# Where four small SBUF buffers lie: the stationary operand of the feed-forwards' down projection

## The chip, the core and the metric

The kernel is one program on one core of a Trainium2 chip. The metric is the device time of one execution in microseconds (us), lower is better. Before the change the median of three runs is 3006.59 us (3006.22 to 3006.69).

## The reference: what is computed

The reference is a stack of transformer layers on 256 tokens of width 1024, all in float32. Four layers of a first block (sliding-window attention, gated linear attention, RWKV-7, sliding-window attention) and one layer of a second block (dilated plus grouped attention) each hold one token mixer and two feed-forwards, so there are ten feed-forwards in all:

```
def swiglu(x, w_in, w_out):
    gate, up = jnp.split(x @ w_in, 2, axis=-1)
    return (jax.nn.silu(gate) * up) @ w_out       # 1024 -> 2 x 2816 -> 1024

for layer in range(DEPTH):
    ff = swiglu(rmsnorm(h, g[0]), ffn_w_in[layer, 0], ffn_w_out[layer, 0])
    h = h + 0.5 * rmsnorm(ff, g[1])
    ...                                           # mixer, then a second feed-forward
```

The second block's feed-forwards are the same with three separate matrices (`ffn1_w1`, `ffn1_w3`, `ffn1_w2` and `ffn2_...`).

## The kernel before, in words

Every engine has a program written out by hand; the order of its instructions is the order of the Python code, and semaphores tie the engines together. Nothing is scheduled or planned by a tool.

**Split numbers.** TensorE multiplies float32r operands. To keep float32 accuracy each operand `a` is split in two float32r parts, `a = high + low`, and a product is taken as high·high + high·low + low·high. Weights arrive by DMA in `raw0` to `raw3`; ScalarE rounds a slot to `high0`/`high1` (`split_high`, L333), VectorE makes `low0`/`low1` as the rest (`split_low`, L337). The turned activation `x_parts` has, for each of the eight 128-row blocks of the model width, 256 tokens of high part and behind them 256 tokens of low part.

**A feed-forward** (`ffn_pe`, `ffn_act`, `ffn_dve`) walks 22 blocks of 128 hidden columns in units q = 0 to 22. Unit q first makes the gate and the up columns of block q: for each of 2 x 8 steps one matmul of 512 columns (L413; weights `high` stationary, `x_parts` moving, both parts at once) and one of 256 columns (L414; `low` stationary, the high part moving). Then it does the down projection of block q-1: for 2 token tiles and 2 halves of the output three matmuls of 512 columns each (L433, L434, L435), 12 in all. There the activation is the stationary operand and the weights are moving:

```
nc.tensor.matmul(o, hid_h[b][:, tok], H[:, w], start=(q == 1), stop=False)
nc.tensor.matmul(o, hid_h[b][:, tok], L[:, w], start=False, stop=False)
last = nc.tensor.matmul(o, hid_l[b][:, tok], H[:, w], start=False, stop=(q == FB))
```

`hid_h[b]` and `hid_l[b]` are the two parts of the activated block, 128 partitions x 256 tokens, two buffers of each (b = (q-1) % 2). VectorE writes them once per unit, `hid_h` at L503 and `hid_l` at L505; it waits first for the down projection two blocks back, and TensorE waits for L505 before L433. Beside `hid_*` nothing here is touched by the change. The mixers don't use `hid_*`.

**Projections of the mixers** (`proj_pe`, L589) have two layouts. With feature-major output the weights are stationary. Token-major ones take `x_parts` as stationary and the weights as moving; the output projections among them stream 512 columns in the same order of three terms (high·high, high·low, low·high) as the down projection does.

**Where buffers lie.** `sb(...)` hands out SBUF from low to high addresses in the order of the calls, without gaps but for a rounding up to 32 bytes. Per partition, in bytes, as the built program has it:

```
buffer            before    after    remainder by 128: before, after
raw0..raw3         16512    same     0
high0, high1       65664    same     0
low0, low1         90240    same     0
x_parts           131200    same     0   (16384 bytes, to 147584)
hid_h0            157888    147584   64, 0
hid_h1            158912    148608   64, 0
hid_l0            159936    149632   64, 0
hid_l1            160960    150656   64, 0
gain0, gain1      147584    151680   0, 0
gain_columns0     155776    159872   0, 0
silu, hidden      155840    159936   64, 64
ident             161984    same     64
mix               167264    same     96
```

Divided by 512, `x_parts` leaves 128, `hid_*` left 192 before and leave 128 after: the 512-byte line of the change's name is counted from the first buffer, which starts at 16512.

Of the kernel before, what the change touches and what calls it, by code (L numbers as in the profile page):

```python
# [6 lines left out]
F32R = mybir.dt.float32r  # L7
# [4 lines left out]
P = 128  # L12
SEQ = 256
# [90 lines left out]
def build(nc, io, out, stages):  # L104
# [49 lines left out]
    with ctx:  # L154
        def sb(name, shape, dt=F32):
            return ctx.enter_context(nc.sbuf_tensor(name, shape, dt))
# [8 lines left out]
        y = sb("y", [P, NT, D])  # L165
        x_parts = sb("x_parts", [P, KB, 2 * SEQ], F32R)
        xh, xl = x_parts[:, :, 0:SEQ], x_parts[:, :, SEQ:2 * SEQ]
        gain = [sb(f"gain{i}", [P, D]) for i in range(2)]
        gain_columns = [sb(f"gain_columns{i}", [P, KB]) for i in range(2)]
        silu = sb("silu", [P, SEQ])  # L170
        hidden = sb("hidden", [P, SEQ])
        hid_h = [sb(f"hid_h{i}", [P, SEQ], F32R) for i in range(2)]
        hid_l = [sb(f"hid_l{i}", [P, SEQ], F32R) for i in range(2)]
        ident = sb("ident", [P, P])
        ones = sb("ones", [P, P])
        squares = sb("squares", [P, 2 * NT])
# [3197 lines left out]
```

## Time and profile before

| | value |
|---|---|
| median of three runs | 3006.59 us (3006.22 to 3006.69) |
| time of the profiled execution | 3007.35 us |
| span of the profiled execution | 3005.4 us |
| TensorE busy with matmuls | 2882.7 us, 96% of the span |
| VectorE, ScalarE, GpSimd busy | 70%, 48%, 3% |
| mean share of the 16 DMA engines | about half (51.7% for the weights' queue) |
| mean granted TensorE clock | 0.988 of full |

The span goes from the first to the last instruction; the profiled execution's own time is 1.95 us longer. In the trace, PE is TensorE's matmul side and PEld its loading of the stationary operand, which runs beside the matmul before it. Records of matmuls overlap, since they are pipelined: a matmul's length includes a latency that the next one hides. What a matmul costs in a dense row is therefore read from start to start, and the time given for one record only by comparison with another of the same shape.

### The profile page before, as it was taken

The numbers are of one execution on the slowest core, as the hardware profiler recorded it, in microseconds if no ns is written. First come the engines' busy times: TensorE is split into PE (matmuls) and PEld (weight loads), VectorE is DVE, ScalarE is ACT, GpSimd is POOL, SyncE is SP. The second block draws the span as 40 slices with busy tenths as digits, with TensorE's granted clock in tenths as the row PEclk, the third lists the DMA queues.
The fourth block names the chain that finished last, engine by engine and source line by source line (L and its number), as shares of the span: only waits on it lengthen the run. The fifth ranks groups of instructions, "written<-read, shape, count | busy, mean of one in ns | idle before, by whom it ended". The sixth has DMA issues, their size and how long they took to land.

```text
span 3005.4 us, 44680 instructions
## 1 busy us (share of the span) xinstructions
PE 2882.7 (96%) x17202; PEld 2491.9 (83%) x17202; DVE 2102.8 (70%) x3035; ACT 1448.9 (48%) x1865; POOL 84.4 (3%) x94
## 2 busy tenths in 40 slices
PE   8998999999999999999999999998999999989998
PEld 7887787888888888888988878876887889978887
DVE  6767677776767777767767777766777775565676
ACT  5445545445544444563444454455445444444443
POOL 0000000000000000100120000000000000000000
PEclk9999999999999999999999999999999999999999
DMA  8643564663456566431016656643656656533662
GB/s 241 207 115 127 173 196 142 210 191 114 133 179 196 157 189 207 121 121 50 1 53 186 196 153 198 185 126 120 189 182 175 189 159 183 183 116 129 200 195 84
DMA packets 614848, 471.24 MB, mean 157 GB/s; under 512 B 40545, under 2 KB 572385, under 8 KB 614708
## 3 DMA queue, kind: packets, MB, share of 16 engines
q1 hardware_dynamic: 614564, 469.31, 51.7%
q8 instruction: 95, 1.56, 0.2%
q14 instruction: 45, 0.37, 0.0%
q10 hardware_dynamic: 144, 0.00, 0.0%
HBM read 466.37 MB, written 1.84 MB: 156 GB/s over the span
## 4 chain that ended last, share of the span: by engine, by line
PE 84%; DVE 8%; ACT 5%; issue 2%; DMA 0%; SPq 0%; PEldq 0%; ACTq 0%; DVEq 0%; PEld 0%
PE pair_bank L413 26%; PE pair_bank L414 14%; PE pair_bank L589 11%; PE out_banks L433 7%; PE out_banks L435 7%; PE out_banks L434 7%; PE out_banks L589 2%; DVE low L337 2%; ACT high L333 2%; PE pair_bank L406 1%; PE pair_bank L2200 1%; PE pair_bank L2188 1%; DVE h L733 1%; PE pair_bank L2184 1%; DVE y L723 1%
## 5 line engine op out<-in xcount | busy, mean ns | idle before, releaser
L337 DVE TENSOR_TENSOR low<-raw,high 128x3072 fp32r<-128x3072 f32 (+2 forms) x328 | 934.7, 2850 | 603.7 <-ACT high L333 602.9
L413 PE MATMUL pair_bank<-x_parts,high 128*128 128x512 f32 x3360 | 1179.1, 393 | 4.4 <-issue 2.4
L414 PE MATMUL pair_bank<-x_parts,low 128*128 128x256 f32 x3520 | 961.9, 280 | 0.0
L333 ACT ACTIVATE high<-raw 128x3072 fp32r<-128x3072 f32 (+2 forms) x328 | 774.0, 2360 | 255.2 <-PE out_banks L435 154.0
L413 PEld LDWEIGHTS pair_bank<-x_parts,high 128*128 128x128 f32 x3360 | 629.6, 187 | 150.3 <-issue 7.8
L414 PEld LDWEIGHTS pair_bank<-x_parts,low 128*128 128x128 f32 x3520 | 655.1, 189 | 10.7 <-DVE low L337 1.1
L463 ACT ACTIVATE sq_scratch<-pair_bank 128x512 f32<-128x512 f32 x220 | 131.6, 598 | 559.1 <-PE pair_bank L414 559.1
L433 PE MATMUL out_banks<-high,hid_h 128*128 128x512 f32 x880 | 348.5, 396 | 9.5 <-DVE hid_l L505 9.5
L434 PE MATMUL out_banks<-low,hid_h 128*128 128x512 f32 x880 | 347.9, 395 | 0.0
L435 PE MATMUL out_banks<-high,hid_l 128*128 128x512 f32 x880 | 347.8, 395 | 0.0
L589 PE MATMUL pair_bank<-high,x_parts 128*128 128x256 f32 x1216 | 232.1, 289 | 4.6 <-DVE x_parts L786 1.6
L589 PE MATMUL pair_bank<-x_parts,high 128*128 128x256 f32 (+2 forms) x1088 | 204.9, 290 | 12.8 <-DVE x_parts L786 5.2
L433 PEld LDWEIGHTS out_banks<-high,hid_h 128*128 128x128 f32 x880 | 165.2, 188 | 52.7 <-issue 13.6
L493 DVE TENSOR_TENSOR sq_scratch<-sq_scratch,pair_bank 128x256 f32<-128x256 f32 x440 | 183.7, 417 | 26.5 <-ACT sq_scratch L463 21.3
L589 PEld LDWEIGHTS pair_bank<-high,x_parts 128*128 128x128 f32 x1216 | 195.6, 195 | 7.0 <-DVE low L337 3.5
L465 ACT ACTIVATE silu<-sq_scratch 128x256 f32<-128x256 f32 x220 | 92.0, 418 | 222.8 <-DVE sq_scratch L495 222.6
L435 PEld LDWEIGHTS out_banks<-high,hid_l 128*128 128x128 f32 x880 | 165.4, 188 | 39.7
L495 DVE TENSOR_TENSOR sq_scratch<-sq_scratch,y 128x256 f32<-128x256 f32 x440 | 187.3, 426 | 15.0
L434 PEld LDWEIGHTS out_banks<-low,hid_h 128*128 128x128 f32 x880 | 165.3, 188 | 29.5
L589 PEld LDWEIGHTS pair_bank<-x_parts,high 128*128 128x128 f32 (+2 forms) x1088 | 171.5, 194 | 17.9 <-DVE low L337 10.1
L589 PE MATMUL pair_bank<-low,x_parts 128*128 128x256 f32 x608 | 173.6, 286 | 0.0
L589 PE MATMUL pair_bank<-x_parts,low 128*128 128x256 f32 (+2 forms) x544 | 156.1, 287 | 0.0
(374 smaller groups left out, 3060.6 us busy)
## 6 DMA issues: line engine op xcount, KB each, us to landing
raw<-in_ffn_w_in_dram SPq DMA_DIRECT2D x352, 512.0 KB
raw<-in_ffn_w_out_dram SPq DMA_DIRECT2D x176, 512.0 KB
raw<-in_ffn_w_dram SPq DMA_DIRECT2D x132, 512.0 KB
raw<-in_w_in_dram SPq DMA_DIRECT2D x32, 1024.0 KB
raw<-in_gla_w_in_dram SPq DMA_DIRECT2D x12, 1024.0 KB
raw<-in_rwkv_w_rkv_dram SPq DMA_DIRECT2D x12, 1024.0 KB
raw<-in_swa_w_qkv_dram SPq DMA_DIRECT2D x10, 1024.0 KB
raw<-in_swa_w_o_dram SPq DMA_DIRECT2D x8, 1024.0 KB
```

The lines of the kernel that those rows point to most:

```text
L333: nc.scalar.activation(high[u % SPLIT][:, lo:w], raw[u % RAW][:, lo:w], ACT.Copy).then_inc(high_ready, count)
L337: nc.vector.tensor_tensor(low[u % SPLIT][:, lo:w], raw[u % RAW][:, lo:w], high[u % SPLIT][:, lo:w].bitcast(F32), ALU.subtract).then_inc(we ...
L413: nc.tensor.matmul(o, H[:, w], x_parts[:, k, :], start=(k == 0), stop=False)
L414: last = nc.tensor.matmul(o[:, 0:SEQ], L[:, w], xh[:, k, :], start=False, stop=(k == KB - 1))
L433: nc.tensor.matmul(o, hid_h[b][:, tok], H[:, w], start=(q == 1), stop=False)
L434: nc.tensor.matmul(o, hid_h[b][:, tok], L[:, w], start=False, stop=False)
L435: last = nc.tensor.matmul(o, hid_l[b][:, tok], H[:, w], start=False, stop=(q == FB))
L463: nc.scalar.activation(lows[:, :, :], halves[:, :, SEQ:2 * SEQ], ACT.Copy).then_inc(lows_copied, 1)
L465: nc.scalar.activation(silu[:, :], sums[:, 0, :], ACT.Silu).then_inc(silu_ready, 1)
L493: nc.vector.tensor_tensor(sums[:, n, :], lows[:, n, :], halves[:, n, 0:SEQ], ALU.add).then_inc(sums_made, 1)
L495: nc.vector.tensor_tensor(sums[:, n, :], sums[:, n, :], scale_rows, ALU.mult).then_inc(sums_ready if n == 0 else sums_made, 1)
L589: last = nc.tensor.matmul(o, a, b, start=(j == 0 and opens), stop=(j == len(terms) - 1 and closes))
```

## The change

Four declarations stand in another place. No instruction, no order, no wait and no size differs: on each of the five engines the rows of the two programs are the same, and only the addresses inside them differ.

```
--- before.py
+++ after.py
@@ -165,12 +165,12 @@
         y = sb("y", [P, NT, D])
         x_parts = sb("x_parts", [P, KB, 2 * SEQ], F32R)
         xh, xl = x_parts[:, :, 0:SEQ], x_parts[:, :, SEQ:2 * SEQ]
+        hid_h = [sb(f"hid_h{i}", [P, SEQ], F32R) for i in range(2)]
+        hid_l = [sb(f"hid_l{i}", [P, SEQ], F32R) for i in range(2)]
         gain = [sb(f"gain{i}", [P, D]) for i in range(2)]
         gain_columns = [sb(f"gain_columns{i}", [P, KB]) for i in range(2)]
         silu = sb("silu", [P, SEQ])
         hidden = sb("hidden", [P, SEQ])
-        hid_h = [sb(f"hid_h{i}", [P, SEQ], F32R) for i in range(2)]
-        hid_l = [sb(f"hid_l{i}", [P, SEQ], F32R) for i in range(2)]
         ident = sb("ident", [P, P])
         ones = sb("ones", [P, P])
         squares = sb("squares", [P, 2 * NT])
```

So `hid_*` come 10304 bytes lower, directly behind `x_parts`; `gain0`, `gain1`, the gain columns, `silu` and `hidden` go up by 4096 bytes, which changes neither their remainder by 128 nor that by 512; everything else stays.

## Rows read from the trace of the kernel before

**Rows 1.** The page: busy times, then by line the chain that ended last.

```profile
PE 2882.7 (96%) x17202; PEld 2491.9 (83%) x17202; DVE 2102.8 (70%) x3035; ACT 1448.9 (48%) x1865; POOL 84.4 (3%) x94
...
PE pair_bank L413 26%; PE pair_bank L414 14%; PE pair_bank L589 11%; PE out_banks L433 7%; PE out_banks L435 7%; PE out_banks L434 7%; PE out_banks L589 2%; DVE low L337 2%; ACT high L333 2%; PE pair_bank L406 1%; PE pair_bank L2200 1%; PE pair_bank L2188 1%; DVE h L733 1%; PE pair_bank L2184 1%; DVE y L723 1%
```

**Rows 2.** Windows of one unit and of 19 units: TensorE busy, granted clock.

```profile
core 0: us, PE busy (x) PEld busy (x) DVE busy (x) ACT busy (x) POOL busy (x), PEclk, DMA share, GB/s
60.00:68.35 8.35, 8.35 (x46) 7.10 (x45) 6.07 (x8) 3.85 (x4) 0.00 (x0) 1.00 0.61 188
...
834.46:850.08 15.62, 15.62 (x70) 12.94 (x69) 7.80 (x5) 7.70 (x8) 0.00 (x0) 1.00 0.68 208
...
341.04:499.76 158.72, 158.72 (x837) 135.63 (x836) 117.39 (x157) 72.29 (x58) 0.00 (x0) 1.00 0.60 182
```

**Rows 3.** Timeline of TensorE in the first feed-forward: start, length, what.

```profile
63.47 0.39 PE L433 MATMUL out_banks<-high,hid_h 128*128 128x512 f32 x1
63.70 0.39 PE L434 MATMUL out_banks<-low,hid_h 128*128 128x512 f32 x1
...
66.27 0.40 PE L413 MATMUL pair_bank<-x_parts,high 128*128 128x512 f32 x1
66.50 0.27 PE L414 MATMUL pair_bank<-x_parts,low 128*128 128x256 f32 x1
66.61 0.40 PE L413 MATMUL pair_bank<-x_parts,high 128*128 128x512 f32 x1
...
71.82 0.39 PE L433 MATMUL out_banks<-high,hid_h 128*128 128x512 f32 x1
```

**Rows 4.** The same view in an output projection, `x_parts` stationary.

```profile
838.12 0.62 PE L589 MATMUL out_banks<-high,x_parts 128*128 128x512 f32 x2
838.57 0.39 PE L589 MATMUL out_banks<-low,x_parts 128*128 128x512 f32 x1
838.80 0.62 PE L589 MATMUL out_banks<-high,x_parts 128*128 128x512 f32 x2
...
849.00 0.61 PE L589 MATMUL out_banks<-high,x_parts 128*128 128x512 f32 x2
```

**Rows 5.** Instructions by tile: count, then length in ns, min/median/max.

```profile
L433 PEld LDWEIGHTS out_banks<-high,hid_h x880: 186/188/188, 29.9 to 2992.9; 128*128 128x128 f32 x176
L433 PE MATMUL out_banks<-high,hid_h x880: 391/394/476, 30.0 to 2993.1; 128*128 128x512 f32 x176
...
L589 PEld LDWEIGHTS out_banks<-high,x_parts x128: 186/188/330, 826.2 to 1586.2; 128*128 128x128 f32 x128
L589 PE MATMUL out_banks<-high,x_parts x128: 387/389/764, 826.2 to 1586.4; 128*128 128x512 f32 x128
```

**Rows 6.** Timeline of RWKV: plain float32 matmuls, stationary in `raw`, then in `mix`.

```profile
1394.76 1.06 PE L2188 MATMUL pair_bank<-raw 128*128 128x128 f32 x8
...
1416.93 1.06 PE L2188 MATMUL pair_bank<-mix 128*128 128x128 f32 x8
```

**Rows 7.** Timeline of a unit near a feed-forward's end: splitting, then the writes of `hid_*`.

```profile
492.06 2.77 ACT L333 ACTIVATE high<-raw 128x3072 fp32r<-128x3072 f32 x1 [0.90 <-PE out_banks L435]
...
494.87 3.36 DVE L337 TENSOR_TENSOR low<-raw,high 128x3072 fp32r<-128x3072 f32 x1 [2.11 <-ACT high L333]
...
500.16 0.39 PE L413 MATMUL pair_bank<-x_parts,high 128*128 128x512 f32 x1
500.36 0.29 DVE L503 CAST hid_h<-hidden 128x256 fp32r<-128x256 f32 x1
...
500.68 0.42 DVE L505 TENSOR_TENSOR hid_l<-hidden,hid_h 128x256 fp32r<-128x256 f32 x1
```

**Rows 8.** Waits of TensorE over the kernel: us in total, times, longest.

```profile
PE out_banks L433 <- DVE hid_l L505: 9.5, 10, 1.1
```

**Rows 9.** Timeline of a feed-forward's last two down projections.

```profile
505.71 0.39 PE L433 MATMUL out_banks<-high,hid_h 128*128 128x512 f32 x1
505.91 0.60 ACT L463 ACTIVATE sq_scratch<-pair_bank 128x512 f32<-128x512 f32 x1 [2.62 <-PE pair_bank L414]
...
509.61 0.47 PE L433 MATMUL out_banks<-high,hid_h 128*128 128x512 f32 x1 [0.93 <-DVE hid_l L505]
```

More of the change, by code:

```diff
@@ L167, in build @@
         xh, xl = x_parts[:, :, 0:SEQ], x_parts[:, :, SEQ:2 * SEQ]
+        hid_h = [sb(f"hid_h{i}", [P, SEQ], F32R) for i in range(2)]
+        hid_l = [sb(f"hid_l{i}", [P, SEQ], F32R) for i in range(2)]
         gain = [sb(f"gain{i}", [P, D]) for i in range(2)]
@@ L171, in build @@
         hidden = sb("hidden", [P, SEQ])
-        hid_h = [sb(f"hid_h{i}", [P, SEQ], F32R) for i in range(2)]
-        hid_l = [sb(f"hid_l{i}", [P, SEQ], F32R) for i in range(2)]
         ident = sb("ident", [P, P])
```

## The prediction

> **What bounds the kernel now.** I read the page's busy times and its chain first. TensorE is busy 96% of the span, and the chain of work that ended last is TensorE for 84%: gate and up matmuls 40% (L413, L414), the down projection 21% (L433 to L435, 7% each) [rows 1]. Then the windows: inside a feed-forward a unit takes 158.72 / 19 = 8.354 us, TensorE has no gap in it, VectorE is busy 117.39 / 158.72 = 74% and the clock is granted in full, 2.4 GHz [rows 2]. So a unit lasts as long as its 44 matmuls, and the question is what one costs from start to start. The timeline gives it: the 12 down matmuls go from 63.47 to 66.27, which is 2.80 / 12 = 233.3 ns each; the 16 pairs of gate and up from 66.27 to 71.82, 5.55 / 16 = 347 ns for 512 and 256 columns together [rows 3].
>
> The view that decides is the same timeline in a mixer's output projection. It streams 512 columns of weights too, with the same three terms in the same order, but its stationary operand is `x_parts`: 48 matmuls from 838.12 to 849.00, 10.88 / 48 = 226.7 ns each, at the same full clock [rows 4, 2]. The difference is 6.7 ns, which is 16 clocks of 2.4 GHz. The records by tile say it again from another side: with `x_parts` a 512-column matmul has min/median 387/389 ns, with `hid_h` 391/394, while the loads of the stationary operand are recorded alike, 188 ns [rows 5]. The pairs fit the smaller figure: 512 + 32 and 256 + 32 clocks are 832 clocks, 346.7 ns, as measured; 512 + 32 clocks are 226.7 ns; the down projection needs 512 + 48. In pairs and output projection every stationary operand begins at a multiple of 128 bytes. `hid_*` begin 64 bytes behind one.
>
> **The change, part by part.**
>
> *The stationary loads of the down projection.* They get the remainder that `x_parts` has, by 128 and by 512. If the address makes the 16 clocks, a down matmul costs 226.7 instead of 233.3 ns. Per unit 12 x 6.67 = 80 ns, and the unit goes from 8.354 to 8.274 us. There are 880 records of L433 [rows 5], four to a block of 12 matmuls, so 220 blocks, 22 to each of the ten feed-forwards.
>
> *What of it is on the path.* In 21 blocks of 22 the next work of TensorE stands ready behind the down projection. The block before the last is different: after it TensorE waits for the last `hid_l`, ten times, 9.5 us in total [rows 8]. That wait ends with VectorE, whose chain starts from the last gate and up matmul (ScalarE at 505.91), ahead of the down block, and ends at 509.46; TensorE starts at 509.61 [rows 9]. A shorter block there only lengthens the wait. So 210 blocks count: 210 x 80 ns = 16.8 us.
>
> *What could be late next.* ScalarE can split the next slot only when L435 has freed one, and both ends move together. In the unit shown ScalarE starts at 492.06, VectorE ends the low part at 494.87 + 3.36 = 498.23, and TensorE wants it at 500.16: 1.9 us of room, against 0.08 us that go [rows 7]. The hidden block is ready at 500.68 + 0.42 = 501.1 and is wanted after the 5.55 us of pairs, at 505.7 [rows 7, 9]. The weights' rate rises by 1%, from 182 GB/s with the DMA engines 60% busy [rows 2]. None of them comes near.
>
> *The other moved buffers.* `gain*`, `silu` and `hidden` keep their remainders, and they are read and written by VectorE and ScalarE beside a TensorE that is the bound. I put them at 0, with at most 0.3 us either way: the feed-forwards' tails are the only place where such an instruction is waited for, three in each of the ten (L499, L503, L505), and with 10 ns on each that is 0.3 us.
>
> *Bounds of the saving.* The trace has no float32r matmul with `hid_*` elsewhere, so the cost after is bounded by the nearest rows. From below: 226.7 ns, the output projection's. From above: 233.3 ns, as now. Between them stands the pitch from a 512-column L413 to its L414, 66.27 to 66.50, 230 ns [rows 3]; but the pair as a whole needs the 32 + 32 clocks, so I take 226.7. Outside these ends a little more could come: the pitches into the block (L414 to L433) and out of it also change by a few ns, at most 10 ns in each of 210, 2.1 us more.
>
> Sum: 16.8 us. The profiled execution took 3007.35 us with a span of 3005.4, so it would be 2990.5 and 2988.6. It lies 0.8 us above the median of the runs; from the median 3006.6 - 16.8 = **2989.8 us**, 0.56% less.
>
> *A page against it.* The trace shows 233.3 and 226.7 ns for one shape at one clock [rows 3, 4]. The Trainium skill, "SBUF — State Buffer", Specifications (TRN2), gives SBUF cachelines of 16 bytes as the grain at which an access pays for crossing; 64 is a multiple of 16, so by that rule the old and the new place are equally good and the time stays. "TensorE: Matmul & The Clock Gate", LDWEIGHTS (loading the stationary operand), has the load cost go by its columns alone, again with no address in it; and Back-to-back issue gap gives about 215.8 ns for 512 columns at full clock, which neither row reaches (no run here shows that value). What such an indifference would do here is the first rival.
>
> **The rivals.**
>
> *1. The address does not matter; the 16 clocks come from how the down projection is built.* It changes the output bank after every third matmul, the output projection after 24; it runs in a loop, the other doesn't; its stationary operand is written by VectorE shortly before. For it: in plain float32 the remainder shows nothing, eight matmuls with the stationary operand in `raw` (remainder 0) and eight with it in `mix` (96) take the same 1.06 us [rows 6]. Against it: those are another kind of matmul, about 112 ns for 128 columns; the pairs run in the same loop at 32 clocks over their columns; and a cost of the bank change would stand at every third matmul, but the first to the second (63.47 to 63.70, no change of bank between) is no shorter than 230 ns either. Time: 3006.6 us.
>
> *2. Half of it.* The down projection in the loop has its own floor at the 230 ns of L413 [rows 3]: 210 x 12 x 3.3 ns = 8.3 us, 2998.3 us. Against it stands that this 230 is followed by 117.
>
> *3. Slower: VectorE now writes next to what TensorE streams.* VectorE writes `hid_h` and `hid_l` (0.29 + 0.42 us) just when TensorE has begun the pairs and streams `x_parts` [rows 7], and now these buffers adjoin. If a write near by slows the stream, 0.71 us of every unit are exposed, 156 us over 220 units. It turns the sign from 80 / 710 = 11% of slowing on; at 20% it costs 31 us and the time is 3006.6 + 31 - 17 = 3021 us. Against it: for 3.36 us of a unit VectorE writes `low`, whose buffers adjoin each other and `high`, while TensorE loads from them, and TensorE stays without a gap [rows 2, 7].
>
> *4. The change doesn't do what it says.* The buffers do not start at a multiple of 512 bytes but 128 behind one. If a full line were needed nothing would move; but `x_parts` has the same remainder and runs at 226.7 ns, so this has little weight and goes into rival 1.
>
> **How the numbers follow.** The forecast has 0.75: one kind of matmul, one shape, one clock, and only the stationary operand's place in common with the change. Rival 1 (with 4) has 0.12, rival 2 0.07, rival 3 0.06. The forecast's own range is 2987 to 2992 (2.1 us more at the low end; at the high end as much, should one block in eight be held by something that I don't see). The range needs 8 in 10, so it takes in rival 2 as well: 2986 to 3000. A difference of 0.2%, 6 us, is about what a measurement tells here: faster 0.82, the same 0.12, slower 0.06.
>
> **What would show it.** In the changed profile L433 to L435 have a median near 389 ns instead of 394, their starts lie 0.227 us apart, and 12 take 2.72 us; the loads stay at 188 ns; 19 units take 157.2 us instead of 158.7; the wait for the last `hid_l` rises from 9.5 to about 10.3 us; L413, L414 and L589 stay. If the pitch stays at 233 ns the address is not the cause. If the pitch falls but the pairs' pitch rises above 347 ns in their first 0.7 us, rival 3 is at work. If the pitch falls to 227 and the time doesn't follow, one of the waits that I called far away is near.

## The result, and the profile after

The changed kernel takes 3014.12 us (median of 12 runs, 3008.74 to 3016.7) against 3006.23 us (12 runs); the ratio is 1.0029 with an interval of 1.0022 to 1.0036. It is 0.29% slower, where 0.56% faster was forecast, and outside the range.

The page after, against [rows 1]: busy times, then two groups of its fifth part.

```profile
PE 2889.4 (96%) x17202; PEld 2495.0 (83%) x17202; DVE 2104.7 (70%) x3035; ACT 1449.5 (48%) x1865; POOL 84.6 (3%) x94
...
L413 PE MATMUL pair_bank<-x_parts,high 128*128 128x512 f32 x3360 | 1196.7, 399 | 4.8 <-issue 2.3
...
L433 PE MATMUL out_banks<-high,hid_h 128*128 128x512 f32 x880 | 345.7, 393 | 10.0 <-DVE hid_l L505 10.0
```

The same two groups of the page of before:

```profile
L413 PE MATMUL pair_bank<-x_parts,high 128*128 128x512 f32 x3360 | 1179.1, 393 | 4.4 <-issue 2.4
...
L433 PE MATMUL out_banks<-high,hid_h 128*128 128x512 f32 x880 | 348.5, 396 | 9.5 <-DVE hid_l L505 9.5
```

So the down projection's matmuls got shorter and the gate and up matmuls, which the change doesn't touch, longer. By tile, against [rows 5], the down matmul moved as forecast:

```profile
L433 PEld LDWEIGHTS out_banks<-high,hid_h x880: 186/188/188, 29.7 to 2999.8; 128*128 128x128 f32 x176
L433 PE MATMUL out_banks<-high,hid_h x880: 387/389/470, 29.9 to 3000.0; 128*128 128x512 f32 x176
```

The windows after, against [rows 2], one unit of the first feed-forward and 19 of the second: 8.39 us, and 159.35 / 19 = 8.387 us, at the full clock.

```profile
60.00:68.39 8.39, 8.39 (x46) 7.16 (x45) 6.11 (x8) 3.85 (x4) 0.00 (x0) 1.00 0.63 190
342.59:501.94 159.35, 159.25 (x837) 135.79 (x837) 117.53 (x158) 72.31 (x58) 0.00 (x0) 1.00 0.60 182
```

The timeline of one unit after, against [rows 3], has it all:

```profile
367.95 0.39 PE L413 MATMUL pair_bank<-x_parts,high 128*128 128x512 f32 x1
368.18 0.28 PE L414 MATMUL pair_bank<-x_parts,low 128*128 128x256 f32 x1
368.29 0.40 PE L413 MATMUL pair_bank<-x_parts,high 128*128 128x512 f32 x1
...
369.00 0.40 PE L413 MATMUL pair_bank<-x_parts,high 128*128 128x512 f32 x1
369.24 0.28 PE L414 MATMUL pair_bank<-x_parts,low 128*128 128x256 f32 x1
369.35 0.40 PE L413 MATMUL pair_bank<-x_parts,high 128*128 128x512 f32 x1
...
373.59 0.40 PE L433 MATMUL out_banks<-high,hid_h 128*128 128x512 f32 x1
373.82 0.40 PE L434 MATMUL out_banks<-low,hid_h 128*128 128x512 f32 x1
...
374.98 0.39 PE L433 MATMUL out_banks<-high,hid_h 128*128 128x512 f32 x1
...
376.34 0.39 PE L413 MATMUL pair_bank<-x_parts,high 128*128 128x512 f32 x1
```

From 374.98 to 376.34 six down matmuls take 1.36 us, 226.7 ns each: the forecast pitch. But the first six behind the pairs take 1.39 us, 232 ns each. All 12 take 2.75 us instead of 2.80. The 16 pairs, 367.95 to 373.59, take 5.64 us instead of 5.55: 352.5 ns a pair, with a 512-column matmul of 0.24 us in every third pair (369.00 to 369.24). Per unit: 51 ns won, 85 lost, 34 ns net; over 210 units 7.1 us, against 7.9 us measured.

That slow pace of the pairs was already in the trace of before. Its timeline in unit q = 2 of the third feed-forward:

```profile
537.15 0.40 PE L413 MATMUL pair_bank<-x_parts,high 128*128 128x512 f32 x1
...
542.10 0.40 PE L413 MATMUL pair_bank<-x_parts,high 128*128 128x512 f32 x1
```

Fourteen pairs in 4.95 us, 353.6 ns each, where [rows 3] have 347. Unit q = 2 of three more of the ten feed-forwards, and q = 1 of six, run at it too. From q = 3 on the pairs of all ten are at 347 ns. So one stretch of code, at one set of addresses and at one clock, has two paces.

The changed kernel's trace shows the opposite step. In its second feed-forward the pairs of q = 2 still have the fast pace, and those of q = 3 the slow one:

```profile
343.23 0.40 PE L413 MATMUL pair_bank<-x_parts,high 128*128 128x512 f32 x1
...
348.43 0.39 PE L433 MATMUL out_banks<-high,hid_h 128*128 128x512 f32 x1
...
351.18 0.39 PE L413 MATMUL pair_bank<-x_parts,high 128*128 128x512 f32 x1
...
356.82 0.40 PE L433 MATMUL out_banks<-high,hid_h 128*128 128x512 f32 x1
```

Fifteen pairs in 5.20 us are 346.7 ns each; sixteen in 5.64 us are 352.5. Between them stands one down projection, the first in which TensorE doesn't wait. Seven of its ten feed-forwards have q = 2 at the fast pace, and in all ten every unit from q = 3 on is slow. In the first two units, where TensorE still waits between pairs and down projection, either pace occurs in both kernels; from q = 3 on the layout decides.

### The profile page after: what moved, and what is told of

It reads as the page before. It is cut to its first block, busy times and chain, and to the rows that moved or that the text cites. A ratio compares the mean times of both kernels' runs of the same rounds, so it can differ in the third digit from the quotient of the medians.

```text
span 3012.2 us, 44680 instructions
## 1 busy us (share of the span) xinstructions
PE 2889.4 (96%) x17202; PEld 2495.0 (83%) x17202; DVE 2104.7 (70%) x3035; ACT 1449.5 (48%) x1865; POOL 84.6 (3%) x94
## 4 chain that ended last, share of the span: by engine, by line
PE 83%; DVE 9%; ACT 5%; issue 2%; DMA 0%; SPq 0%; PEldq 0%; ACTq 0%; DVEq 0%; PEld 0%
PE pair_bank L413 26%; PE pair_bank L414 14%; PE pair_bank L589 11%; PE out_banks L433 6%; PE out_banks L434 6%; PE out_banks L435 6%; PE out_banks L589 2%; DVE low L337 2%; ACT high L333 2%; PE pair_bank L406 1%; PE pair_bank L2200 1%; PE pair_bank L2188 1%; DVE h L733 1%; PE pair_bank L2184 1%; DVE y L723 1%
## 5 line engine op out<-in xcount | busy, mean ns | idle before, releaser
L413 PE MATMUL pair_bank<-x_parts,high 128*128 128x512 f32 x3360 | 1196.7, 399 | 4.8 <-issue 2.3
L414 PE MATMUL pair_bank<-x_parts,low 128*128 128x256 f32 x3520 | 964.5, 281 | 0.0
L413 PEld LDWEIGHTS pair_bank<-x_parts,high 128*128 128x128 f32 x3360 | 631.9, 188 | 163.5 <-issue 8.3
L414 PEld LDWEIGHTS pair_bank<-x_parts,low 128*128 128x128 f32 x3520 | 655.4, 189 | 9.0 <-DVE low L337 1.1
L433 PE MATMUL out_banks<-high,hid_h 128*128 128x512 f32 x880 | 345.7, 393 | 10.0 <-DVE hid_l L505 10.0
L589 PE MATMUL pair_bank<-high,x_parts 128*128 128x256 f32 x1216 | 232.9, 289 | 4.6 <-DVE x_parts L786 1.6
L589 PE MATMUL pair_bank<-x_parts,high 128*128 128x256 f32 (+2 forms) x1088 | 206.3, 291 | 12.8 <-DVE x_parts L786 5.2
L433 PEld LDWEIGHTS out_banks<-high,hid_h 128*128 128x128 f32 x880 | 165.2, 188 | 52.3 <-issue 14.0
L589 PEld LDWEIGHTS pair_bank<-high,x_parts 128*128 128x128 f32 x1216 | 196.2, 195 | 7.1 <-DVE low L337 3.5
L589 PEld LDWEIGHTS pair_bank<-x_parts,high 128*128 128x128 f32 (+2 forms) x1088 | 172.8, 195 | 18.0 <-DVE low L337 10.1
L589 PE MATMUL pair_bank<-low,x_parts 128*128 128x256 f32 x608 | 174.0, 286 | 0.0
L589 PE MATMUL pair_bank<-x_parts,low 128*128 128x256 f32 (+2 forms) x544 | 156.8, 288 | 0.0
```

Source lines behind the costliest of these rows:

```text
L413: nc.tensor.matmul(o, H[:, w], x_parts[:, k, :], start=(k == 0), stop=False)
L414: last = nc.tensor.matmul(o[:, 0:SEQ], L[:, w], xh[:, k, :], start=False, stop=(k == KB - 1))
L589: last = nc.tensor.matmul(o, a, b, start=(j == 0 and opens), stop=(j == len(terms) - 1 and closes))
```

## The experiments

All but e5 and e6 only reorder declarations; the program is otherwise the one before. Remainders are by 512 bytes. Two operands are called in step when they leave the same remainder, and out of step when they don't. `gain_columns` (64 bytes) serves as the spacer. "Down" is from the first L433 of a unit to the next L413, "pairs" from there to the next L433; both are medians over 180 units, "unit" the mean over 190, from the starts in each trace. They repeat within 0.01 us per unit where two kernels have the same remainders (before and e2, changed and e1, e3 and e11, e16 and e17), much better than whole runs: the span without 190 units (mixers and edges) lay between 1411 and 1424 us in these profiles. Two numbers stand where the units alternate; in e7 half of the units of either parity have each. The last column is the ratio to the kernel before with its 95% interval, or the time in us.

| kernel | hid_h | hid_l | high | low, x_parts | down, us | pairs, us | unit, us | time |
|---|---|---|---|---|---|---|---|---|
| before | 192 | 192 | 128 | 128 | 2.798 | 5.555 | 8.353 | 3006.2 |
| changed | 128 | 128 | 128 | 128 | 2.747 | 5.640 | 8.387 | ratio 1.0029 |
| e1 | 128 | 128 | 128 | 128 | 2.747 | 5.640 | 8.388 | 1.0023 (1.0014 to 1.0033) |
| e2 | 192 | 192 | 128 | 128 | 2.798 | 5.555 | 8.351 | 0.9998 (0.9988 to 1.0007) |
| e3 | 128 | 192 | 128 | 128 | 2.770 | 5.550 | 8.320 | 0.9991 (0.9981 to 1.0001) |
| e4 | 192 | 128 | 128 | 128 | 2.802, 2.777 | 5.552, 5.550 | 8.339 | 0.9993 (0.9984 to 1.0003) |
| e5 | 128 | 128, 192 | 128 | 128 | 2.777 | 5.550 | 8.327 | 0.9991 (0.9982 to 1.0) |
| e6 | 192, 128 | 128 | 128 | 128 | 2.793 | 5.640 | 8.434 | 3023.85, one run |
| e7 | 160, 224 | 160, 224 | 128 | 128 | 2.80 to 2.81 | 5.55 or 5.65 | 8.405 | 3022.4, one run |
| e8 | 256 | 256 | 128 | 128 | 2.776, 2.796 | 5.644, 5.551 | 8.383 | 3012.25, one run |
| e9 | 192 | 192 | 192 | 192 | 2.747 | 5.640 | 8.387 | 3009.13, one run |
| e10 | 192 | 192 | 128 | 128, 192 | 2.803 | 5.643 | 8.445 | 3017.59, one run |
| e11 | 128 | 192 | 128 | 128 | 2.770 | 5.550 | 8.320 | 0.9986 (0.9977 to 0.9995) |
| e12 | 192 | 128 | 192 | 128 | 2.774 | 5.446 | 8.221 | 0.9917 (0.9903 to 0.9931) |
| e13 | 128 | 128 | 192 | 128 | 2.789, 2.804 | 5.597, 5.450 | 8.317 | 3001.57, one run |
| e14 | 128 | 128 | 128 | 192, 128 | 2.784, 2.779 | 5.550, 5.653 | 8.386 | 3007.86, one run |
| e15 | 192 | 192 | 192 | 128 | 2.784 | 5.609 | 8.393 | 1.0026 (1.0015 to 1.0037) |
| e16, e17 | 128 | 192 | 192 | 128 | 2.767 | 5.439 | 8.207 | 0.99 (0.9884 to 0.9917) |

(The two remainders of e5 and e6 are those of the first and the second token tile, those of e7 of its two buffers, those of e10 and e14 of low and x_parts. e16 is one run, 2975.76 us; the ratio is e17's.)

**Place or remainder: e1 and e2.** Theory A: the pairs' pace is handed on by the down projection's loads. Theory B, rival 3 of the prediction: `hid_*` next to `x_parts` disturb.

```
e1_far_aligned, from before      e2_near_64, from before
   x_parts                          x_parts
   gain                          +  gain_columns
-  gain_columns                  +  hid_h, hid_l
   silu, hidden, hid_h, hid_l       gain
+  gain_columns                  -  gain_columns
                                    silu, hidden
                                 -  hid_h, hid_l
```

> The gain columns are declared behind hid_*, so hid_* stay 10 KB from x_parts (157824) but begin at a multiple of 128 bytes. In the changed kernel a down matmul fell from 233 to about 227 ns (once five matmuls had passed), but the pairs of gate and up behind it rose from 347 to 352.5 ns, all 16 alike; the unit went from 8.354 to 8.387 us. Theory A (the pace of the pairs is carried over from the down matmuls ahead of them: the misaligned loads had put TensorE's loading and streaming in a favourable step): the place doesn't matter, only the remainder, so this is as the changed kernel: unit 8.387 us, about 3014 us. Theory B (hid_* next to x_parts disturbs the stream of x_parts): down 227 and pairs 347, unit 8.27 us, about 2990 us.

> The gain columns (64 bytes) are declared between x_parts and hid_*: hid_* are next to x_parts (147648) but begin 64 bytes behind a multiple of 128, as in the kernel before. Theory A: as the kernel before, down 233, pairs 347, unit 8.354 us, about 3006 us. Theory B: down 233 and pairs 352.5, unit about 8.43 us, about 3023 us.

Both came out as A has it, each to 2 ns per unit of the kernel that it should equal: far away but in step is as slow as the changed kernel, adjoining but out of step is as before. That refutes rival 3.

**Which loads set the pace: e3 to e6.** In e3 and e4 the spacer stands between the two parts, behind `x_parts`:

```
e3_low_part_64:   x_parts, hid_h, gain_columns, hid_l, gain, silu, hidden
e4_high_part_64:  x_parts, hid_l, gain_columns, hid_h, gain, silu, hidden
```

> Behind x_parts come hid_h (multiple of 128), then the gain columns, then hid_l (64 behind one). Of each three down matmuls one has a misaligned load, and it is the last before the pairs. Theory A, if the last load before the pairs sets their step: pairs 347, down 8 x 6.7 ns shorter, unit 8.30 us, about 2995 us. Theory A, if the step needs several such loads in a row: pairs 352.5, unit about 8.41 us, 3019 us. Theory B: pairs 352.5 in any case, 3019 us.

> As the one before with the parts exchanged: hid_l at a multiple of 128, hid_h 64 behind one; two of three down matmuls have a misaligned load, the last before the pairs has an aligned one. Theory A, if the last load sets the step: pairs 352.5, down 4 x 6.7 ns shorter than before, unit about 8.41 us, 3019 us. Theory A, if most of the loads do: pairs 347, unit 8.33 us, 3001 us. Theory B: 3019 us.

In both the pairs kept 347 ns. e3's unit fell to 8.320 us, somewhat more than half of the way to the 8.30 expected, and its time is 3003.42 us where 2995 was expected. e4 contradicted "the last load alone": the one right ahead of the pairs is in step, and they stayed at 347. e5 and e6 put a gap of 16 columns inside one tensor, so that one token tile of it is out of step (`hid_l` second tile in e5, `hid_h` first tile in e6). The edit of e5, cut; VectorE's write and TensorE's read take the two tiles from the gapped tensor, and four small buffers are packed into one, which no other kernel has:

```
-        hid_l = [sb(f"hid_l{i}", [P, SEQ], F32R) for i in range(2)]
+        hid_l_all = sb("hid_l", [P, 2 * 2 * P + 16], F32R)
+        hid_l = [bass.AP(hid_l_all[:, :].tensor, hid_l_all[:, :].offset + i * P, [[2 * 2 * P + 16, P], [2 * P + 16, NT], [1, P]]) for i in range(2)]
...
```

> hid_* behind x_parts and at multiples of 128, but the second token half of hid_l 64 bytes behind one (16 columns of gap inside the tensor). Only matmuls 9 and 12 of the 12 of a down projection have a misaligned load, the last one before the pairs among them. With all of hid_l misaligned the unit was 8.320 us and the pairs 347 ns. Carried step, set by the last load before the pairs: pairs 347, unit 8.29 to 8.31 us, 2993 to 2997 us. If it needs a misaligned load in every three: pairs 352.5, unit about 8.39 us, 3014 us.

> The opposite: only the first token half of hid_h is 64 bytes behind a multiple of 128, so matmuls 1, 2, 4 and 5 have a misaligned load and the last seven before the pairs an aligned one. Carried step, set by the last loads: pairs 352.5 as in the changed kernel, unit 8.39 to 8.40 us. If the pairs only need some misaligned load ahead of them in the unit: pairs 347, unit about 8.32 us.

Timelines of one unit each, first L433, first L413, next L433 (numbered one lower here), of e5 and then of e6:

```profile
372.29 0.39 PE L432 MATMUL out_banks<-high,hid_h 128*128 128x512 f32 x1
...
375.06 0.39 PE L412 MATMUL pair_bank<-x_parts,high 128*128 128x512 f32 x1
...
380.62 0.39 PE L432 MATMUL out_banks<-high,hid_h 128*128 128x512 f32 x1
```

```profile
374.72 0.39 PE L432 MATMUL out_banks<-high,hid_h 128*128 128x512 f32 x1
...
377.52 0.39 PE L412 MATMUL pair_bank<-x_parts,high 128*128 128x512 f32 x1
...
383.16 0.39 PE L432 MATMUL out_banks<-high,hid_h 128*128 128x512 f32 x1
```

In e5 the pairs take 5.56 us, in e6 5.64. Two loads out of step late in the down projection hold the pairs at the fast pace, four early ones don't. Both units are longer than expected (8.327 us against 8.29 to 8.31, 8.434 against 8.39 to 8.40), and e5's time is 3004.04 us, 7 us above its range. In e6 the slow pairs and a slow down projection come together. e4 and e6 differ in the second tile of `hid_h`, matmuls 7, 8, 10 and 11: with it out of step the pairs are fast, without it slow. So the pace is handed over from what runs late in the down projection.

**Line or distance: e7 to e10.** e7 puts the two buffers 32 and 96 bytes behind a multiple of 128, e8 puts all of them 128 bytes past `x_parts`' remainder:

```
e7: x_parts, gain_columns0, hid_h0, hid_l0, gain_columns1, squares, hid_h1, hid_l1, root, gain, ...
e8: x_parts, gain_columns, squares, root, hid_h, hid_l, gain, rstd, idle, silu, hidden, ...
e9, from before:                    e10, from the changed kernel:
   raw                                 h, y
+  gain_columns                     +  gain_columns
   high, low, h, y, x_parts, gain      x_parts, hid_h, hid_l, gain
-  gain_columns                     -  gain_columns
```

> hid_h0 and hid_l0 begin 32 bytes, hid_h1 and hid_l1 96 bytes behind a multiple of 128, so units of one parity have the one and those of the other the other remainder. If a multiple of 64 is what an aligned load needs, both are misaligned by the same and the units are 8.35 us or longer, alike; if the cost goes by the remainder to 128, the two parities differ. Under both the pairs stay at 347 ns if any misaligned load ahead of them sets the favourable step.

> All of hid_* at a multiple of 128 bytes, but with remainder 256 by 512 where x_parts has 128 (the gain columns and two small buffers stand between). If 128 is the grain: as the changed kernel, pairs 352.5, unit 8.387 us, about 3013 us. If the line of 512 shared with x_parts is what matters: as the kernel before, down 233, unit 8.354 us.

> From the kernel before: the gain columns (64 bytes) are declared ahead of high0, so that high, low, x_parts and hid_* all leave 192 by 512; hid_* keep their very addresses. If what counts is the remainder of the stationary operand alone (an absolute line), all float32r loads are now misaligned: pairs and L589 lose too, the unit is 8.7 us or longer. If what counts is where the stationary operand lies against the moving one, modulo 512, all are in step as in the changed kernel: down 2.75 us, pairs 5.64 us, unit 8.387 us, about 3013 us, although no address of hid_* differs from before.

> From the changed kernel: the gain columns are declared ahead of x_parts, so x_parts and hid_* leave 192, the weights (high, low) 128. Stationary and moving operand are 64 bytes out of step in the pairs and in the down projection. Absolute line: pairs at 347 or 352.5 ns (stationary high, low unmoved), down 233: unit 8.35 to 8.43 us. Relative position: every matmul costs some 6.7 ns more: pairs about 360 ns, unit 2.80 + 5.76 = 8.56 us, about 3050 us.

e7 refuted my "pairs stay at 347 if any load is out of step": half of its units had the slow pace, though the down projection takes the same in both parities to 3 ns. e8 refuted the grid of 128 bytes that the prediction argued with: at a multiple of 128, but 128 away from the others by 512, the down projection does not reach 2.747 us. Its units alternate between the two paces, and in three of its ten feed-forwards the parities are exchanged. A pace that follows the last unit and not the buffer is one that is handed on. e9 is the cleanest of all. There `hid_*` keep the very addresses of before, and everything that they meet moves by 64:

```profile
371.44 0.40 PE L433 MATMUL out_banks<-high,hid_h 128*128 128x512 f32 x1
...
374.19 0.39 PE L413 MATMUL pair_bank<-x_parts,high 128*128 128x512 f32 x1
...
379.83 0.40 PE L433 MATMUL out_banks<-high,hid_h 128*128 128x512 f32 x1
```

2.75 us and 5.64 us, the changed kernel's numbers. So it is how the buffers lie to each other that counts, and no absolute line. Distances of 0, 32, 64, 96 and 128 bytes by 512 were tried; 256 was not, so whether the effect repeats every 512 bytes or every 256 is not shown.

e10 took the pairs out of step too. Its feed-forward alone doesn't tell the two theories apart: the unit, 8.445 us, lies between their forecasts, and the pairs' 352.7 ns are not the 360 that I had expected from a relative position. The output projections decide. In e9 and e10 `x_parts`, stationary there, leaves the same 192, and only the weights differ (192 and 128). First e9, then e10, 54 matmuls each at the full clock:

```profile
838.26 0.39 PE L589 MATMUL out_banks<-low,x_parts 128*128 128x512 f32 x1
...
850.50 0.39 PE L589 MATMUL out_banks<-low,x_parts 128*128 128x512 f32 x1
```

```profile
838.37 0.40 PE L589 MATMUL out_banks<-low,x_parts 128*128 128x512 f32 x1
...
850.97 0.40 PE L589 MATMUL out_banks<-low,x_parts 128*128 128x512 f32 x1
```

12.24 / 54 = 226.7 ns in step, 12.60 / 54 = 233.3 ns out of it. The 256-column matmuls of the mixers go the other way: the median pitch falls from 120 ns to 116 to 118. In e10's own pairs a 256-column matmul doesn't get shorter (117 to 123 ns), so this holds for those rows only.

**Was the rest of e3 lost to the gains: e11.** The layout of e3 with `squares` and `root` behind `hid_l`, so that `gain` is at a multiple of 128 again.

> The layout with hid_h in step and hid_l 64 bytes out of it, again, but with gain0 and gain1 back at a multiple of 128 (squares and root stand ahead of them). In the first run of the layout the unit was 8.320 us, 0.033 us less than before, so 210 units should bring 6.9 us, and the runs showed 2.6 us with an interval of 3 either way. If the misplaced gains took the rest: about 2999 us (ratio 0.9977). If part of the saving is not passed on to the end of the kernel: 3003 us again (0.999).

3001.69 us, 0.9986: 4.2 us less than before, with an interval of 1.5 to 6.9 that holds the 2.7 us of e3 and, just, the 6.9 us of the units. Whether the gains matter these runs can't tell.

**A layout from a theory: e12 to e17.** The theory of the next load: while one matmul streams, the stationary operand of the next is loaded, and the pitch goes by how these two lie to each other; 512 columns are faster in step, 256 out of it.

```
e12: raw, low, h, y, x_parts, hid_l, gain_columns, high, hid_h, gain, silu, hidden, ...
e13: raw, low, h, y, x_parts, hid_h, hid_l, gain_columns, high, gain, ...
e14: raw, high, h, y, x_parts, hid_h, hid_l, gain_columns, low, gain, ...
e15: raw, low, h, y, x_parts, gain_columns, high, hid_h, hid_l, gain, ...
e16, e17: raw, low, h, y, x_parts, hid_h, gain_columns, high, hid_l, gain, ...
```

> Remainders by 512: low, x_parts and hid_l 128, high and hid_h 192 (high is declared behind x_parts). With x_parts and hid_* 64 out of step, 512-column matmuls cost 233 instead of 227 ns, but 256-column ones about 117 instead of 120. Theory: while a matmul streams, the next stationary operand is loaded, and the pitch goes by how these two stand to each other. Here the 512-column stream of x_parts runs beside the load of low (in step), the 256-column one beside the load of high (out of step), and in the down projection each stream beside a load in step with it. So: pairs 227 + 117 = 344 ns or less, down 12 x 227 = 2.72 us, unit 8.19 to 8.24 us, 2970 to 2985 us. If the slow mode of the pairs (352.5) turns up instead: unit 8.37 us, 3010 us. If each pitch goes by the matmul's own two operands: pairs 233 + 120, down 233 for L434 and L435: unit 8.43 us or more, 3022 us.

> high alone at 192, hid_h and hid_l at 128 with low and x_parts. Theory as for e12_high_and_hid_h_192: pairs the same 344 ns or less; in the down projection the streams of high run beside loads of hid_h that are out of step: 8 of 12 at 233: 2.77 us; unit 8.24 to 8.29 us, 2980 to 2993 us.

> The counterpart: low alone at 192, everything else at 128. By the theory the 512-column stream of x_parts runs beside loads of low that are out of step (233) and the 256-column one beside loads of high in step (120): pairs 353 ns or more, 5.65 us; down 4 of 12 out of step, 2.75 us; unit 8.40 us, about 3017 us. If the pitch goes by a matmul's own operands instead: 512 columns in step (227), 256 out of step (117), pairs 344 ns, unit about 8.26 us.

e12 was inside its forecast: 2980.16 us, pairs at 340 ns, 227 + 113. e13 reached that pace in every second unit only (its unit, 8.317 us, and its time are above its forecast), and one of its ten feed-forwards has the parities exchanged, as in e8. e14 never did (347 and 353 ns, where the next load had 353 and the own operands 344). So e12's 340 ns speak for the next load against a matmul's own operands, which had 353; e14 fits neither. For the down projection of e12 the theory fails: 2.774 us instead of 2.72. Two more kernels were to tell:

> As e12_high_and_hid_h_192, but hid_l at 192 too (gain columns and high stand between x_parts and hid_*). There the pairs came to 340 ns as the theory of the next load has it, but 12 down matmuls took 2.774 us, not 2.72. Next load: streams of high run beside loads of hid_h in step, streams of low beside loads of hid_l out of step, 4 of 12: down 2.75 to 2.78 us. A matmul's own operands: L434 alone is out of step, 4 of 12 as well, against 8 of 12 in e12: down 2.75 us, less than e12's. Both: pairs 5.45 us, unit 8.20 to 8.23 us, 2976 to 2983 us.

> hid_l at 192 with high, hid_h at 128 with low and x_parts: the opposite of e12. Next load: every stream of the down projection runs beside a load that is out of step: down 2.80 us, unit 8.25 to 8.27 us. A matmul's own operands: L434 and L435 in step, L433 alone out: down 2.75 us, unit 8.20 us.

e15's unit, in which nothing but `hid_l` differs by remainder from e12's, and then e17's:

```profile
373.58 0.40 PE L433 MATMUL out_banks<-high,hid_h 128*128 128x512 f32 x1
...
376.37 0.40 PE L413 MATMUL pair_bank<-x_parts,high 128*128 128x512 f32 x1
...
381.98 0.40 PE L433 MATMUL out_banks<-high,hid_h 128*128 128x512 f32 x1
```

```profile
369.36 0.39 PE L433 MATMUL out_banks<-high,hid_h 128*128 128x512 f32 x1
...
372.13 0.39 PE L413 MATMUL pair_bank<-x_parts,high 128*128 128x512 f32 x1
372.36 0.28 PE L414 MATMUL pair_bank<-x_parts,low 128*128 128x256 f32 x1
372.47 0.39 PE L413 MATMUL pair_bank<-x_parts,high 128*128 128x512 f32 x1
...
377.57 0.39 PE L433 MATMUL out_banks<-high,hid_h 128*128 128x512 f32 x1
```

e15 missed by 30 us: its pairs take 351 ns, a second pace. It isn't lost from the start: in five of its ten feed-forwards the pairs of q = 1 run at 340 ns, in three also those of q = 2, and from q = 3 on all are slow. e12 does the reverse: seven of ten have q = 2 at 350 ns or more, and from q = 3 on all are at 340. The pairs' own operands have the same remainders in both; only `hid_l` in the down projection between them differs by remainder. That is the hand-over once more. e16's down projection, 2.767 us, is between the 2.75 and the 2.80 that were to decide, so it decides nothing. But it is the best layout of all, and I timed it again:

> The layout of e16_high_and_hid_l_192 again, timed. Its one run took 2975.8 us with a unit of 8.207 us, pairs 340 ns and down 2.767 us. 210 units at 0.146 us less than before are 30.6 us: 2972 to 2979 us, ratio about 0.990, and the same unit to 0.01 us. If the pairs' mode were a matter of chance in each execution, the runs would scatter by up to 35 us; so far each layout kept its mode in all ten feed-forwards.

2975.57 us (4 runs, 2975.0 to 2975.74), ratio 0.99 (0.9884 to 0.9917), 1.0% less than before, and the same unit. 210 x 0.146 us = 30.7 us, 30.5 us measured. The first two units differ between the two executions of this kernel (in the second feed-forward q = 1 takes 350 ns a pair in e16 and 340 in e17); from q = 3 on the pace belongs to the layout, not to chance.

## Why the prediction was wrong

- *"What bounds the kernel now"*: right. A unit lasts as long as its 44 matmuls, before, after and in every experiment.
- *"If the address makes the 16 clocks, a down matmul costs 226.7 instead of 233.3 ns"*: right once the row runs by itself (374.98 to 376.34). Rival 1, that the address doesn't matter, is refuted by e1, where only addresses differ; e9 shows that the place relative to the other buffers is meant.
- *"Per unit 12 x 6.67 = 80 ns"*: mis-sized. It was 51 ns, since the first six behind the pairs still take 232 ns. 226.7 ns came from a row of 48 equal matmuls [rows 4]; here the row is 12 long and comes from something else. For this row rival 2, half of it, was the nearest.
- *The step that failed: "L413, L414 and L589 stay."* The sum held only the instructions whose addresses changed, and put the pairs at nothing. L589 did stay (227 ns in its 512-column rows before and after). The pairs went from 347 to 352.5 ns, 85 ns per unit, and turned the sign. What stood in its place is a hand-over: the out-of-step loads of the down projection had been putting the pairs at their fast pace, unit after unit, and the in-step ones put them at the slow one (343.23 to 356.82 above). e4, e5 and e6 show that its late loads do it.
- *"In pairs and output projection every stationary operand begins at a multiple of 128 bytes"*: true, and the wrong property. e8 has it for `hid_*` and is not fast. What they share is that stationary and moving operand leave the same remainder by 512 (e9, and the output projections of e9 and e10).
- *Rival 3* had the sign right and the cause wrong (e1, e2). Its mark, pairs above 347 ns in their first 0.7 us, would not have told it from the hand-over: all 16 are slower.
- *"What could be late next"*: right that nothing was. The wait for the last `hid_l` rose from 9.5 to 10.0 us where 10.3 was expected, as 51 ns per block have it: 9.5 + 10 x 0.051.

The Trainium skill, "TensorE: Matmul & The Clock Gate", Step-by-step: what each phase is for, says that stationary and moving operand have two independent SBUF read ports, so that loading the next operand takes nothing from the running matmul. The traces here don't fit that in full: with every instruction alike, the pitch of one 512-column matmul is 227 or 233 ns depending on how the two operands lie to each other (the output projections of e9 and e10). The Trainium skill, "SBUF — State Buffer", Specifications (TRN2), has 16-byte lines; shifts of 64 bytes, which are a whole number of them, changed the unit here from 8.353 to 8.207 us (e17).

Open: what in the hardware makes the two paces, and by which rule a down projection leaves the pairs at one or the other. The next-load theory gives the pairs of e12 and e16 but not those of e15, half of those of e13 and e14, and it is 54 ns too low for the down projection of e12 and 33 too high for that of e16. Also open: e3 and e5 won some 2.7 us in the runs where their units say 6.9 and 5.5; their intervals end at 5.7 and 5.4, just short of that.

## What to carry to other kernels

A change to one stretch of a dense row of matmuls can change the pace of the stretch behind it, so price the whole period, not only the instructions that you edit; and look in the trace of before for stretches of equal code with two paces, they say what there is to lose. Where float32r matmuls are the bound, how stationary and moving buffers lie to each other, in steps of 64 bytes, is a free parameter worth 1% here. No theory of mine gave the best layout beforehand, so try a few and read the period of one loop in one profile of each: it repeats to 0.1%, while whole runs need many rounds.

## What the runs showed of the hardware

- With full clock and stationary loads of 128 x 128 float32r beside each stream, a 512-column matmul in a long row of equal ones takes 227 ns in step and 233 out of step (output projections of e9 and e10). In the pairs of before it takes 230 to 233 ns although it is in step.
- A 256-column one goes the other way in the mixers: 120 ns in step, 116 to 118 in e10. In the pairs it is not so simple: 112 to 118 ns in step before, 117 to 123 out of step in e10, and 113 in e12 and e17, where only the next load is out of step.
- The pace of a periodic row has more than one state. In step the pairs run at 347 or 352.5 ns, with `high` out of step at 340 or 351. Which one they take is set by the down projection of 12 matmuls ahead of them: it can hold a pace for all units from q = 3 on (before, changed, e12, e15) or exchange it in every unit (e8, e13).
- The median length recorded for the loads stays at 187 to 188 ns in all of this; only starts tell.
